# One store of seven operands per up chunk, and five edits around it, in a decoder trunk kernel

## The reference, cut to what matters

```
def memory_cross_attention(xq, m, w_kv):      # k, v = split(m @ w_kv); softmax(xq k^T) v, 4 heads
def sq_relu_mlp(h, w_up, w_down):             # u = square(relu(h @ w_up)); return u @ w_down
```

## Time and profile before

| | us |
|---|---|
| median of three runs | 2402.2 (2399.67, 2402.2, 2403.47) |
| profiled execution, its time | 2399.22 |
| its span | 2397.4 |
| mean granted TensorE clock | 0.997 of full speed |
| PE busy | 2372.4 |
| DVE busy | 1605.2 |
| ACT busy | 1158.4 |
| POOL busy | 293.4 |

### The profile page before, as it was taken

How to read it: one execution, slowest core, us unless ns; L and a number is a source line. 1 busy time by engine, 2 the same in 40 slices (tenths; PEclk the granted TensorE clock), 3 DMA queues, 4 the chain that set the end, 5 groups by cost and what they waited for, 6 DMA issues and landing times.

```text
span 2397.4 us, 30002 instructions
## 1 busy us (share of the span) xinstructions
PE 2372.4 (99%) x11004; PEld 1979.8 (83%) x11004; DVE 1605.2 (67%) x2408; ACT 1158.4 (48%) x1922; POOL 293.4 (12%) x309
## 2 busy tenths in 40 slices
PE   9999999999999999999999999999999999999998
PEld 8888888888878888888888888888887888888887
DVE  5678866888877775546646769567797666554545
ACT  5645554346655454444534345533575554543333
POOL 0043200331000000003000431023210000000001
PEclk9999999999999999999999999999999999999999
DMA  9875677756377668674544626654453544585553
GB/s 339 336 262 205 225 260 294 262 173 232 119 253 269 233 242 322 242 278 176 193 176 176 245 88 223 242 208 162 174 186 128 180 153 158 183 336 187 198 189 141
DMA packets 212866, 518.36 MB, mean 216 GB/s; under 512 B 12433, under 2 KB 104977, under 8 KB 188145
## 3 DMA queue, kind: packets, MB, share of 16 engines
q1 hardware_dynamic: 212288, 516.36, 59.5%
q10 hardware_dynamic: 432, 0.07, 0.0%
HBM read 377.98 MB, written 138.41 MB: 215 GB/s over the span
## 4 chain that ended last, share of the span: by engine, by line
PE 91%; DVE 4%; DMA 2%; issue 1%; ACT 1%; POOL 0%; SPq 0%; DVEq 0%; ACTq 0%; POOLq 0%
PE banks L3144 27%; PE banks L3146 26%; PE banks L3145 26%; PE banks L3355 3%; PE banks L3395 1%; PE banks L3327 1%; PE banks L3304 1%; PE banks L3401 1%; PE banks L3379 1%; DVE w_lo L2889 1%; DMA gain_fin<-in_w_down 1%; PE banks L3317 1%; PE banks L3413 0%; DMA raw<-in_w_out 0%; DMA raw<-in_w_up 0%
## 5 line engine op out<-in xcount | busy, mean ns | idle before, releaser
L3144 PE MATMUL banks<-h_hi,w_hi 128*128 128x512 f32 x896 | 357.6, 399 | 6.1 <-DVE part_b L2937 5.6
L3146 PE MATMUL banks<-h_hi,w_lo 128*128 128x512 f32 x896 | 350.1, 391 | 0.0
L3144 PE MATMUL banks<-w_hi,u_hi 128*128 128x512 f32 x896 | 349.4, 390 | 0.0
L3145 PE MATMUL banks<-h_lo,w_hi 128*128 128x512 f32 x896 | 349.1, 390 | 0.0
L3146 PE MATMUL banks<-w_hi,u_lo 128*128 128x512 f32 x896 | 348.6, 389 | 0.0
L3145 PE MATMUL banks<-w_lo,u_hi 128*128 128x512 f32 x896 | 348.6, 389 | 0.0
L2955 DVE TENSOR_TENSOR w_lo<-raw,w_hi 128x1024 fp32r<-128x1024 f32 x112 | 140.4, 1253 | 204.6 <-ACT w_hi L2063 204.6
L2063 ACT ACTIVATE w_hi<-raw 128x1024 fp32r<-128x1024 f32 x112 | 118.4, 1058 | 293.8 <-PE banks L3144 254.2
L3144 PEld LDWEIGHTS banks<-h_hi,w_hi 128*128 128x128 f32 x896 | 169.0, 189 | 41.5 <-ACT w_hi L1994 6.4
L3144 PE MATMUL banks<-s_hi,w_hi 128*128 128x512 f32 x512 | 199.7, 390 | 0.6 <-DVE w_lo L2889 0.6
L3146 PE MATMUL banks<-s_hi,w_lo 128*128 128x512 f32 x512 | 199.2, 389 | 0.0
(11 more groups left out here) (338 smaller groups left out, 4707.1 us busy)
## 6 DMA issues: line engine op xcount, KB each, us to landing
u_raw<-u_kept SPq DMA_DIRECT2D x56, 1024.0 KB, 7.1
u_kept<-u SPq DMA_DIRECT2D x32, 1024.0 KB, 4.9
raw<-w_mix SPq DMA_DIRECT2D x32, 1024.0 KB, 4.8
raw<-in_w_up SPq DMA_DIRECT2D x30, 1024.0 KB, 5.5
w_hi<-w_in_hi SPq DMA_DIRECT2D x29, 1024.0 KB, 4.8
w_lo<-w_in_lo SPq DMA_DIRECT2D x29, 1024.0 KB, 7.5
u_kept<-u SPq DMA_DIRECT2D x32, 768.0 KB, 3.3
raw<-in_w_down SPq DMA_DIRECT2D x24, 1024.0 KB, 5.7
```

What stands on the lines that cost most here:

```text
L3144: after_chunk(pe.matmul(to, left[0], right[0], start=start, stop=False, skip_group_check=goes_on))
L3145: pe.matmul(to, left[0], right[1], start=False, stop=False, skip_group_check=goes_on)
L3146: return pe.matmul(to, left[1], right[0], start=False, stop=stop, skip_group_check=goes_on)
```

## The change

1. `AHEAD` is 25 instead of 28: three fewer matmuls of ones at the start (L3238), whose result nothing reads.
2. The first keys of the memory: the weights' split, ACT's and DVE's, and the products that use it go in quarters instead of halves.
3. Two of the twelve early mixes, those at (0, "keys", 5) and (0, "out", 0), leave the mixers; the up stage of m = 0 now takes 22 instead of 20, two in each chunk from 3 to 13.
4. In the even mixers `scale_column` (DVE, L2790) goes behind the out product's last additions but one, and the two first `next_h_high` of ACT behind the squares.
5. In the up stage's first chunks DVE adds M7 ahead of the weight splits of the step, and makes a chunk's sums one step later.
6. A chunk's u goes to DRAM in one transfer of seven operands, 1792 KB, when squares and sums are there; `part_relus`, `u_sums` and all loads that wait for it wait for this one.

```diff
-EARLY_MIX_AT = {(0, "keys", 5): 0, (0, "silu", 13): 1, (0, "out", 0): 2, (1, "gates", 0): 3, (1, "k", 1): 4, (1, "k", 3): 5,
...
+EARLY_MIX_AT = {(0, "silu", 13): 0, (1, "gates", 0): 1, (1, "k", 1): 2, (1, "k", 3): 3, (1, "keys", 2): 4,
...
             def store_u(m, c):
 
                 sp.wait_ge(*square_ready.at(m, UP_DONE.index(c)))
-                sp.dma_start(u_kept[:, 0:3, c, :], u[:, 0:3, :]).then_inc(u_stored.sem, 16)
-
-            def store_u_sums(m, c):
                 sp.wait_ge(*u_sums_ready.at(m, UP_DONE.index(c)))
-                sp.dma_start(u_kept[:, 3:OPERANDS, c, :], u[:, 3:OPERANDS, :]).then_inc(u_sums_stored.sem, 16)
+                sp.dma_start(u_kept[:, :, c, :], u[:, 0:OPERANDS, :]).then_inc(u_stored.sem, 16)
...
-                    if at - 1 in UP_ENDS:
-                        store_u(m, UP_ENDS[at - 1])
                     if at - 2 in UP_ENDS:
-                        store_u_sums(m, UP_ENDS[at - 2])
+                        store_u(m, UP_ENDS[at - 2])
...
-                if n % 2 == 0:
-                    for k in range(2):
-                        scale_column(n + 1, k)
                 next_chunk(c_out + 6)
...
                 add_product("M3")
+                if n % 2 == 0:
+                    for k in range(2):
+                        scale_column(n + 1, k)
...
                     if at:
-                        dve.wait_ge(*u_sums_stored.at(m, at - 1))
+                        dve.wait_ge(*u_stored.at(m, at - 1))
...
                     if at < FIRST_STEPS:
                         continue
+                    if name == "M7" and c != 2:
+
+                        add_part(c, "M7")
                     if at > FIRST_STEPS:
                         up_low_and_sums(m, at + UP_LEAD)
-                    if name == "M7" and c != 2:
-                        add_part(c, "M7")
-                    elif name == "M4":
+                    if name == "M4":
                         add_part(c, "M3")
-                    if at - 2 in UP_ENDS:
-                        u_sums(UP_ENDS[at - 2])
+                    if at - 3 in UP_ENDS:
+                        u_sums(UP_ENDS[at - 3])
...
+                parts = 2 if i else 4
+                for part in range(parts):
+                    half = 2 * part // parts
+                    if i or part % 2:
+                        pe.wait_ge(*hi_split.early(PIECES * i + half))
+                        pe.wait_ge(*lo_split.early(PIECES * i + half))
+                    else:
+                        pe.wait_ge(quarter_hi, half + 1)
+                        pe.wait_ge(quarter_lo, half + 1)
```

More of the change, by code:

```diff
@@ L67 @@
 PIECES = 2
-AHEAD = 28
+AHEAD = 25
 HALF = BLOCK // 2
@@ L140 @@
 MIX_PLACES, GAIN_PLACE, GATE_PLACES = 3, 3, (4, 5)
-EARLY_PLACES = (3, 3, 3, 3, 4, 5, 3, 4, 5, 3, 4, 3)
+EARLY_PLACES = (3, 3, 4, 5, 3, 4, 5, 3, 4, 3)
 EARLY_MIX = len(EARLY_PLACES)
-EARLY_MIX_AT = {(0, "keys", 5): 0, (0, "silu", 13): 1, (0, "out", 0): 2, (1, "gates", 0): 3, (1, "k", 1): 4, (1, "k", 3): 5,
[L144 to L148, removed]
+EARLY_MIX_AT = {(0, "silu", 13): 0, (1, "gates", 0): 1, (1, "k", 1): 2, (1, "k", 3): 3, (1, "keys", 2): 4,
+                (1, "keys", 3): 5, (1, "keys", 6): 6, (1, "silu", 9): 7, (1, "keys", 11): 8, (1, "silu", 13): 9}
+DOWN_MIX_AT = {UP_AT[FIRST_UPS + (j - EARLY_MIX) // 2, "M1"] + (0, 4)[j % 2]: j for j in range(EARLY_MIX, DOWN_MIX)}
 ALL_MIX_PLACES = EARLY_PLACES + tuple(j % MIX_PLACES for j in range(DOWN_MIX - EARLY_MIX))
@@ L671, in build @@
         first_half_loaded = sem("first_half_loaded")
+        quarter_hi, quarter_lo = sem("quarter_hi"), sem("quarter_lo")
         first_x_loaded = sem("first_x_loaded")
@@ L1114, in _ @@
             half_mix_work = {
[L1115 to L1122, removed]
+                (0, 13): [(half_mix_load, 0)], (0, 16): [(half_mix_store, 0)],
+                (1, 1): [(half_mix_load, 1)], (1, 4): [(half_mix_store, 1), (half_mix_load, 2), (half_mix_load, 3)],
+                (1, 5): [(half_mix_load, 4)], (1, 7): [(half_mix_store, 2), (half_mix_store, 3)],
+                (1, 8): [(half_mix_load, 5), (half_mix_load, 6)], (1, 9): [(half_mix_store, 4), (half_mix_store, 5)],
+                (1, 10): [(half_mix_load, 7), (half_mix_load, 8)], (1, 11): [(half_mix_store, 6)],
+                (1, 12): [(half_mix_store, 7)], (1, 13): [(half_mix_store, 8), (half_mix_load, 9)],
+                (1, 15): [(half_mix_store, 9)]}
             def load_out(n, i):
@@ L1244, in load_down @@
                 sp.dma_start(as_kblocks(raw, slot, DEPTH), down_weights(name, quarter)).then_inc(down_loaded[slot].sem, 16)
-                stored = u_stored if operand < S1 else u_sums_stored
-                sp.wait_ge(*stored.at(m, UP_DONE.index(DEPTH * quarter + DEPTH - 1)))
+                sp.wait_ge(*u_stored.at(m, UP_DONE.index(DEPTH * quarter + DEPTH - 1)))
                 if s == 0 and m:
@@ L1579, in _ @@
                 act.wait_ge(memory_loaded[p], 16)
[L1580 to L1588, removed]
+                for quarter in (2 * p, 2 * p + 1):
+                    for k in range(2 * quarter, 2 * quarter + 2):
+                        nc.scalar.activation(memory_hi[:, k, :], memory[:, k, :], ACT.Copy,
+                                             scale=gain_mem[:, k:k + 1]).then_inc(hi_part.sem, 1)
+                    at = slice(quarter * CHUNK // 4, (quarter + 1) * CHUNK // 4)
+                    if quarter % 2:
+                        nc.scalar.activation(w_hi[:, 0, at], raw[:, 0, at], ACT.Copy).then_inc(hi_split.sem, 1)
+                        continue
+                    if p == 0:
+                        act.wait_ge(first_half_loaded, 16)
+                    else:
+                        act.wait_ge(*raw_loaded[0].early(0))
+                    nc.scalar.activation(w_hi[:, 0, at], raw[:, 0, at], ACT.Copy).then_inc(quarter_hi, 1)
             first_split_hi(1)
@@ L1960, in mixers @@
                 if n % 2 == 0:
-                    for k in range(2, KG):
+                    for k in range(KG):
                         next_h_high(k)
@@ L2293, in _ @@
             for p in range(2):
[L2294 to L2303, removed]
+                for quarter in (2 * p, 2 * p + 1):
+                    for k in range(2 * quarter, 2 * quarter + 2):
+                        dve.wait_ge(*hi_part.early(k))
+                        nc.vector.scalar_tensor_tensor(
+                            out=memory_lo[:, k, :], in0=memory[:, k, :], scalar=gain_mem[:, k:k + 1],
+                            in1=memory_hi[:, k, :].bitcast(F32), op0=ALU.mult, op1=ALU.subtract)\
+                            .then_inc(memory_low, 1)
+                    at = slice(quarter * CHUNK // 4, (quarter + 1) * CHUNK // 4)
+                    if quarter % 2:
+                        dve.wait_ge(*hi_split.early(p))
+                    else:
+                        dve.wait_ge(quarter_hi, p + 1)
+                    nc.vector.tensor_tensor(w_lo[:, 0, at], raw[:, 0, at], w_hi[:, 0, at].bitcast(F32),
+                                            ALU.subtract).then_inc(lo_split.sem if quarter % 2 else quarter_lo, 1)
             first_split_lo(1)
@@ L3207, in memory_keys @@
                 wh, wl = as_kblocks(w_hi, i, KD), as_kblocks(w_lo, i, KD)
-                for half in range(2):
-                    pe.wait_ge(*hi_split.early(PIECES * i + half))
-                    pe.wait_ge(*lo_split.early(PIECES * i + half))
+                parts = 2 if i else 4
[4 more added lines that the diff above has]
+                        pe.wait_ge(*lo_split.early(PIECES * i + half))
+                    else:
+                        pe.wait_ge(quarter_hi, half + 1)
+                        pe.wait_ge(quarter_lo, half + 1)
                     for f in range(2):
-                        for k in range(half * KD // 2, (half + 1) * KD // 2):
+                        for k in range(part * KD // parts, (part + 1) * KD // parts):
                             if i == 0 and f == 0:
```

5 lines of the change are left out of this document (removed).

## The result

The changed kernel takes 2416.3 us (2415.45 to 2419.37, four runs) against 2400.93 beside it (2399.6 to 2403.47): 15.4 us slower, ratio 1.0068 [1.0053, 1.0083]. The forecast was 2407.5, 5.5 us slower. Its profiled execution has a span of 2417.6 us and took 2419.37 us, 3 us above the median of its runs.

What follows compares the result with a forecast made beforehand. PE was taken as the bound, busy 2372.4 of 2397.4 us. Lost 11.0 less gained 5.5 made 5.5 us slower: 2404.7 profiled, 3.0 more for the median, stated as 2407.5; range 2397 to 2417.

Steps and rivals of the forecast that it cites:

- The gains: Start and mixers, outside the MLPs: shorter or removed PE waits win 5.5 us, with bounds from 4 to 6.4.
- the second and third wait of the earlier trace: Mixers: PE's waits of 2.04 and 1.51 us go once two early mixes leave, winning 2.0 and 1.5 us.
- the 1.35: Start: PE's wait ahead of 11.24 for a split that now goes in quarters; gain taken as 0.5, from 0 to 1.35.
- The wait on the copy of chunk 3's M1: Up stage, m = 0: PE stands 6.8 us before M6 of chunk 3, as ACT's relus wait for the store.
- The next turns of u: Up stage to chunk 5: turns of 15 us (14 in m = 1) lag; loses 3.4 us, and 0.4 in m = 1.
- The pace that I set the turns against: Up stage: chunks' ends five steps or 13.6 us apart up to chunk 3, and 19 us after.
- rival (A): Early turns, m = 0: the store meets other transfers, lands in 10.1 us; 9 us on top, about 2417; chance 0.15.
- The slow clock behind the first wait: Up stage, behind PE's wait at M6 of chunk 3: a lower clock loses 1.8 us in each MLP.
- The down stage: Last store 2.2 us later, but the stage begins with other chunks' operands: nothing lost, at most 2.2 us each.
- (B): Up stage: store lands in 4 to 5 us and turns keep up; 1 us faster, about 2401; chance 0.22.
- (C): Up stage, both MLPs: the wait for the store does not reach PE; about 2387.5 or 2397.3 us; chance 0.13.
- the two rules of the Trainium skill: Stores of u: larger transfers use bandwidth better; splitting lets work begin sooner when DMA is mostly idle, taken to hold here.

Runs made afterwards that it cites:

- e10: Kernel before with the start, split, mix and even-mixer changes only: two stores and DVE's old order in the up stage's first chunks; 2396.35 us, ratio 0.9976.
- e5: Changed kernel with DVE making chunk 3's sums ahead of chunk 4's M7 addition, the mixes' instructions and a weight split; 2409.2 us, ratio 1.0038.
- e6: Changed kernel with 26 matmuls, whose result nothing reads, put on PE ahead of M6 of chunk 3; 2415.31 us, ratio 1.0065.
- e2: Kernel before with only the one 1792 KB store behind the sums added; 2413.8 us, ratio 1.0056.
- e4: Changed kernel with DVE's old order: sums at the old step, M7 added behind the weight splits; the one store stays; 2409.68 us, ratio 1.0038.
- e8: Changed kernel run once more, nothing altered; 2416.42 us, ratio 1.0067 to the kernel before.
- e3: Changed kernel with two transfers, 768 and 1024 KB, both issued behind the sums, relus waiting for the first alone; 2400.14 us, ratio 0.9993.

## Why the prediction was wrong in size

**Right:** the sign and the mechanism. The gains: 4.8 us measured (e10) for 5.5. At 164.44 and 252.38, the matmuls of the second and third wait of the earlier trace rows, PE no longer waits:

```profile
164.44 0.38 PE L3356 MATMUL banks<-queries,keys 128*128 128x256 f32 x1
...
252.38 0.47 PE L3138 MATMUL banks<-w_hi,mem_hi_e 128*128 128x512 f32 x1
```

At the start the 1.35 became a new wait of 0.72 at 28.87 for a later split, so 0.5 was left, as taken. (The lower bound of the gains, written as 4, is 4.5 by the terms that are given for it.) The wait on the copy of chunk 3's M1 was forecast at 6.8 us and was 6.87; ACT was forecast to stand on the store, and stood 6.58 us.

**The step that failed** is "The next turns of u": "I count relus 670.2 + 3 turns of 15 = 715.2", and turns of 14 in m = 1. With their slow clock these turns were to lose 3.4 + 0.4 = 3.8 us; they lost 6.2 + 4.3 = 10.5. The three turns took 48.0 us in m = 0 instead of 45, and 46.8 in m = 1 instead of 42 (relus at 1849.79 and 1896.54). Two things made them longer.

In m = 0 it was DVE's work. I had built the turn from its own links and put "other DVE work in between up to three" beside it without looking which. For chunk 3 it is an addition, a mix and a split, 3.8 us after the squares in the trace, and e5, which takes only these away, wins 7.1 us. The same rows, in the same order, stood in the trace of before, where I read DVE's order only at the first place:

```profile
700.64 0.69 DVE L2937 TENSOR_TENSOR part_b<-banks,part_b 128x512 f32<-128x512 f32 x1 [4.33 <-PE banks L3146]
...
703.44 0.69 DVE L2947 TENSOR_TENSOR u<-u 128x512 f32<-128x512 f32 x1
```

In m = 1 it was mostly the landing. I took 6.2 us for all stores there because m = 1 has no mixes; that held for the first of the four, and the next three took 7.1. Each of these three has a load of up weights (`raw`, 1024 KB) under way beside it, and the first has no other transfer. With 0.9 us more, a turn of 14 is nearly the 15.3 of e6. Over the whole changed kernel, the 21 stores with another transfer under way landed in 7.1 to 7.4 us; of the 11 without, ten took 6.15 to 6.35 and one 7.98. In the traces of e2, e4, e5, e6 and e8, which have the one store as well, six of over a hundred with another transfer under way do not fit; they landed in 6.2 to 6.5. So this is an order found in traces, not a test.

The pace that I set the turns against was misread too, though no sum uses it. In before, the relus of chunks 1, 0, 3, 4 and 5 begin 15.9, 16.3, 11.1 and 19.0 us apart, not 13.6 up to chunk 3 and 19 after. The turn of chunk 3's u, which got the most DVE work, has the least room.

The time lies inside the range of 2397 to 2417, but that is luck: the range reached so far for the sake of rival (A), which did not come.

**Mis-sized terms beside it.** The slow clock behind the first wait, 1.8 us in the prediction, was 2.4 us in m = 0 and 3.0 in m = 1; behind the second wait, where I had 0.9 in m = 0 and none in m = 1, it was 1.7 and 1.6. The down stage was counted as nothing with a bound of 2.2 each. PE waits 1.27 us there, and again in e8 (1.25), for the split of an operand whose load is issued right behind the last store (at 931.20, behind 929.87). Behind 1792 KB it lands after 12.2 us, behind the 1024 KB of before after 10.1:

```profile
945.89 0.47 PE L3138 MATMUL banks<-w_hi,u_hi 128*128 128x512 f32 x1 [1.27 <-DVE u_lo L2954]
```

**Rivals.** (A) the crowd: no store of the early turns took 10 us; the size came near 2417 for another reason. (B) quick landing: none was below 6.1. (C) the wait does not reach PE: it did. By the two rules of the Trainium skill weighed in the prediction ("Perfetto Trace Analysis", section "DMA Optimizations"), the one on splitting is borne out: 768 KB landed 3.4 us after issue in e3, 1792 KB 7.1 us after, and the kernel with the split is 16 us faster, although the DMA engines are not mostly idle there (share 0.72 in 660 to 680 of the changed kernel). The one on larger transfers shows nothing here: together the two pieces took 6.8 us.

What stays open: whether it is the other transfer that makes 1792 KB land in 7.1 instead of 6.2 us, since no run moved it away; what the one store of 7.98 us waited for; and whether the waits in the mixer of block 3 belong to edits 1 to 4.

## What to carry to other kernels

With a single buffer, the next writer may begin only when the store out of it has landed; merging that store with data that comes later lengthened the whole turn of the buffer here. Follow such a turn through every engine's written order for as many turns as it is tight, not only through the first: what stands between two links on another engine is part of the turn. And an edit that pays with one version of a wait (edit 5: -8.4 us) can cost with another (+6.6 us), so try it together with what it will meet.

## What the runs showed of the hardware that I had not expected

One transfer of 1792 KB was no faster than two of 768 and 1024 KB issued together (7.1 against 6.8 us until the last has landed), and with the two the early part is known 3.7 us sooner. Alone, the 1792 KB landed in 6.2 us in most cases; beside another transfer, in 7.1. The slow clock behind a wait cost 1.7 and 1.5 us of PE's work behind the waits of 2.8 and 2.7 us before, and 2.4 and 3.0 us behind the waits of 6.9 and 6.0 us. It was absent where PE multiplied through most of the wait (granted clock 1.00 against 0.83 in 660 to 680). Yet keeping the clock up was worth 1 us of 2416, since PE was not what the next 40 us waited for.
